# Two transformer blocks on one core: the differential-attention stage takes its norms by TensorE and one table, the sparse stage hands its roots to GpSimd

## The reference

```python
x = rms_norm(x, final_norm)                     # end of the first block
h = rms_norm_2(x, norm_mix[0])                  # directly behind it: a second norm of the result
q, k, v = split(h @ diff_w_in)                  # 8 heads; q and k normed in 64s, rotated
a = softmax(q1 k1) - lam * softmax(q2 k2)       # causal by chunks of 64
o = rms_norm_2(a @ v, subln_g) * (1 - lam_init); x = x + o @ diff_w_out
...
c_q, k, v, k_idx, w_idx = split(rms_norm_2(x, norm_mix[1]) @ dsa_w_in)
q = norm_rope(c_q @ w_uq); q_idx = rope(c_q @ w_uq_idx)
score = sum_h w_idx * relu(q_idx k_idx)         # masked
valid = top_k(score, 128)                       # per row; attention runs over these alone
```

## Time and profile before

| | |
|---|---|
| time, median of 3 runs | 2650.74 us (2647.53 to 2655.13) |
| the profiled execution: its own time, its span | 2656.82 us, 2654.7 us |
| PE busy | 2449.1 us, 92% |
| ACT, DVE, POOL busy | 906.6, 854.5, 1139.8 us |
| mean granted clock of TensorE | 0.958 |

### The profile page before, as it was taken

One profiled execution on the slowest core, in us unless ns is written; L12 is line 12 of the kernel. 1 busy time (PEld: TensorE's weight loads), 2 busy tenths in 40 slices (PEclk: granted clock), 3 DMA queues, 4 the chain that ended last, 5 costly groups with the idle time before them and its releaser, 6 DMA issues.

```text
span 2654.7 us, 27035 instructions
## 1 busy us (share of the span) xinstructions
PE 2449.1 (92%) x11136; PEld 1970.7 (74%) x11136; DVE 854.5 (32%) x1458; ACT 906.6 (34%) x1296; POOL 1139.8 (43%) x916
## 2 busy tenths in 40 slices
PE   7999999898887999999798679999999879999999
PEld 5888876687764788888586457888886657788887
DVE  3222117453123322200643733102024875420211
ACT  4222224221332422222554644313235245431331
POOL 6444434423631544444642125454454702444442
PEclk9999999989999999999898789999999889999999
DMA  4222222212310233222121003223321100232322
GB/s 134 96 95 95 96 95 72 72 32 98 124 65 16 95 95 95 96 95 96 64 79 64 1 21 91 95 96 99 103 80 65 64 33 17 70 105 96 96 95 79
DMA packets 148589, 210.66 MB, mean 79 GB/s; under 512 B 6121, under 2 KB 116978, under 8 KB 148466
## 3 DMA queue, kind: packets, MB, share of 16 engines
q1 hardware_dynamic: 148466, 208.93, 24.3%
HBM read 206.82 MB, written 2.10 MB: 79 GB/s over the span
## 4 chain that ended last, share of the span: by engine, by line
PE 75%; DVE 12%; ACT 5%; POOL 4%; issue 2%; DMA 2%; SPq 0%; POOLq 0%; ACTq 0%; DVEq 0%
PE ps L1248 22%; PE ps L1249 22%; PE ps L1250 22%; POOL wlo L711 2%; POOL sq L724 2%; PE ps L1865 1%; ACT whi L808 1%; DVE c_work L2528 1%; DVE c_best L2527 1%; PE ps L1841 1%; PE ps L1465 1%; PE ps L1851 1%; PE ps L1535 1%; PE ps L1302 1%; PE ps L1590 1%
## 5 line engine op out<-in xcount | busy, mean ns | idle before, releaser
L711 POOL TENSOR_TENSOR wlo<-raw,whi 128x512 fp32r<-128x512 f32 x776 | 1014.5, 1340 | 1327.2 <-ACT whi L808 1327.2
L808 ACT ACTIVATE whi<-raw 128x2048 fp32r<-128x2048 f32 (+1 forms) x195 | 371.2, 1905 | 779.4 <-DMA raw<-in_mlp_w 326.8
L1248 PE MATMUL ps<-hh,whi 128*128 128x512 f32 x1512 | 600.1, 397 | 26.7 <-DVE hl L1970 17.5
L1249 PE MATMUL ps<-hl,whi 128*128 128x512 f32 x1512 | 592.3, 392 | 0.0
L1250 PE MATMUL ps<-hh,wlo 128*128 128x512 f32 x1512 | 591.9, 391 | 0.0
L1248 PEld LDWEIGHTS ps<-hh,whi 128*128 128x128 f32 x1512 | 286.5, 189 | 104.1 <-issue 36.8
L1250 PE MATMUL ps<-gh,wlo 128*128 128x512 f32 x864 | 336.1, 389 | 0.0
L1248 PE MATMUL ps<-gh,whi 128*128 128x512 f32 x864 | 336.1, 389 | 0.0
L1249 PE MATMUL ps<-gl,whi 128*128 128x512 f32 x864 | 336.1, 389 | 0.0
L1249 PEld LDWEIGHTS ps<-hl,whi 128*128 128x128 f32 x1512 | 286.7, 190 | 59.8 <-issue 1.8
L1250 PEld LDWEIGHTS ps<-hh,wlo 128*128 128x128 f32 x1512 | 286.2, 189 | 60.2
(11 more groups left out here) (405 smaller groups left out, 2732.6 us busy)
## 6 DMA issues: line engine op xcount, KB each, us to landing
raw<-in_mlp_w SPq DMA_DIRECT2D x64, 1024.0 KB, 5.5
raw<-in_ffn_w_gate SPq DMA_DIRECT2D x22, 1024.0 KB, 5.1
raw<-in_ffn_w_up SPq DMA_DIRECT2D x22, 1024.0 KB, 5.2
raw<-in_ffn_w_down SPq DMA_DIRECT2D x22, 1024.0 KB, 4.8
raw<-in_w_in SPq DMA_DIRECT2D x13, 1024.0 KB, 5.2
raw<-in_diff_w_in SPq DMA_DIRECT2D x12, 1024.0 KB, 5.0
raw<-in_xattn_w_kv SPq DMA_DIRECT2D x8, 1024.0 KB, 5.0
raw<-in_dsa_w_in SPq DMA_DIRECT2D x8, 1024.0 KB, 4.9
```

The lines of the kernel that those rows point to most:

```text
L711: nc.gpsimd.tensor_tensor(wlo[i][:, c], raw[i][:, c], whi[i][:, c].bitcast(F32), ALU.subtract).then_inc(s_lo, 1)
L808: nc.scalar.activation(whi[i][:, 0:width(made[0])], raw[i][:, 0:width(made[0])], ACT.Copy)\
L1248: nc.tensor.matmul(dst, w_hi, x_hi, start=start, stop=False)
L1249: nc.tensor.matmul(dst, w_hi, x_lo, start=False, stop=False)
```

## The change

In the entry ACT loads one table set, which serves Ln and Exp, and squares each tile once, into eight tiles `a_xsq` of their own; POOL adds nothing there. PE sums the squares with 32 small matmuls whose moving side `gsq` has two columns, a one and the squared gain. Both norms come out of one Ln and one Exp on a 128x8 tile, since the second mean square follows from both sums. The factor as a tile of rows is made on PE, from `ident` scaled by it, right ahead of the first `turn_rows`, and DVE copies it to `rstd` after group 0; the 8 multiplications of `xT` come after group 3. In the attention `squares` and `row_sums` move ahead in step 1 and `factors` to step 2 of a head, and the turns of heads 6 and 7 move into the output projection. In the sparse stage the sum of squares on PE moves behind half of block b+1, the Newton step to POOL, two insertions of the query projection ahead of the loop, the block b+6 too, POOL splits b+9 before `scaled(2)`, and the mask takes one instruction. The diff, cut:

```diff
+Q_STEPS = (4, 9, 14, 19, 24, 29)
...
             def scaled(g, rows, gain):
 
-                pool.wait_ge(s_cst, g + 1)
+                y, w, u = c_rs[:, g, :], c_w[:, g, :], c_u[:, :]
+                pool.wait_ge(s_rrs2, g + 1)
+                if g:
+                    pool.wait_ge(s_cny, 4 * g)
+                nc.gpsimd.tensor_tensor(u, y, y, ALU.mult).then_inc(s_cny, 1)
...
+                nc.gpsimd.tensor_tensor(u, w, u, ALU.mult).then_inc(s_cny, 1)
+                nc.gpsimd.tensor_scalar(u, u, 1.5, None, ALU.add).then_inc(s_cny, 1)
+                nc.gpsimd.tensor_tensor(y, u, y, ALU.mult).then_inc(s_cny, 1)
+                pool.wait_ge(s_cny, 4 * g + 4)
...
                 scaled(1, c_rowb, "dsa_q_norm_2")
-                split_to(b + 8)
+                split_to(b + 9)
                 scaled(2, c_rowc, "dsa_q_norm_2")
...
-                split_to(b + 1)
-                e = E_DIFF
-                for t in range(1, KT):
-                    pool.wait_ge(s_esq, 8 * e + t + 1)
-                    if t > 1:
-                        pool.wait_ge(s_eacc, 7 * e + t - 1)
-                    first = sg[:, 0, :] if t == 1 else sq[:, 0, :]
-                    nc.gpsimd.tensor_tensor(sq[:, 0, :], first, sg[:, t % 4, :], ALU.add).then_inc(s_eacc, 1)
-                    pool.wait_ge(s_esq2, t + 1)
-                    if t > 1:
-                        pool.wait_ge(s_eacc2, t - 1)
-                    first = t1[:, 0, :] if t == 1 else sq[:, 1, :]
...
                     if p.entry == E_DIFF:
-                        if t >= 2:
-                            act.wait_ge(s_eacc2, max(t - 2, 1))
-                        nc.scalar.activation(t1[:, t % 2, :], xT[:, t, :], ACT.Square, scale=col("final_norm", t))\
-                            .then_inc(s_esq2, 1)
+                        nc.scalar.activation(a_xsq[:, t, :], xT[:, t, :], ACT.Square).then_inc(s_esq, 1)
...
                 prep_to(b + 1)
+                nc.scalar.preload_act_table_set(LN_SET)
                 entry(diff_entry)
                 prep_to(b + 2)
                 act.wait_ge(s_ehalf, E_DIFF + 1)
-                rsqrt(dr[:, 0:4], dr[:, 4:8], s_erstd)
-                act.wait_ge(s_f2, 1)
-                rsqrt(dr[:, 8:12], dr[:, 4:8], s_fr2)
-                act.wait_ge(s_fh, 1)
-                rsqrt(rstd[:, :], t1[:, 0, :], s_fr)
+                rsqrt(dr[:, 0:8], dr[:, 8:16], s_erstd)
                 act.wait_ge(s_rr, 1)
...
-                    if qt == 3 and h:
+                    if qt == 1 and h:
+                        squares(h - 1)
+                    if qt == 2 and h:
                         factors(h - 1)
                     if u < 29:
                         exponents(u + 3)
-                    if qt == 1 and h:
-                        squares(h - 1)
                     if u == 16:
                         prep_to(b + DIFF_BLOCKS + 1)
...
+                for st in range(2):
+                    put_rows(G_Q0, st, c_rowb[:, st, :], c_sq0)
                 put_rows(G_K0, 3, c_rowa[:, 3, :], a_sq, factor(3))
                 row_rstd2(0)
+                prep_to(b + 6)
...
-                    if v % 4 == 3:
-                        g, st = divmod(v // 4, ST)
+                    if v in Q_STEPS:
+                        g, st = divmod(2 + Q_STEPS.index(v), ST)
...
-                    if v in (7, 19):
-                        prep_to(b + 6 + v // 16)
-                turned(20, 4, lambda c: a_kT[:, c, :])
+                    if v == 20:
+                        prep_to(b + 7)
                 row_rstd2(1)
                 row_rstd2(2)
                 prep_to(b + 8)
+                turned(20, 4, lambda c: a_kT[:, c, :])
                 for st in range(ST):
                     put_rows(G_K1, st, c_rowa[:, st, :], a_sq, factor(st))
-                prep_to(b + 9)
+                    if st == 1:
+                        prep_to(b + 9)
...
-                rsqrt(c_rs[:, g, :], newton[:, 0, 0:32], s_rrs2)
+                rsqrt(c_rs[:, g, :], c_w[:, g, :], s_rrs2)
...
+                        if tail is not None and j == 0 and k == 6:
+                            tail()
...
-                pe.wait_ge(s_eacc, 7 * E_DIFF + 7)
-                pe.wait_ge(s_eacc2, 7)
+                pe.wait_ge(s_esq, 8 * E_DIFF + 8)
...
-                for i in range(2):
-                    for st in range(ST):
-                        c = 8 * i + 2 * st
-                        r = nc.tensor.matmul(ps[:, 7, c:c + 2], sq[:, i, ts(st, P)], ones[:, 0:2],
-                                             start=True, stop=True)
+                for st in range(ST):
+                    for t in range(KT):
+                        r = nc.tensor.matmul(ps[:, 7, 2 * st:2 * st + 2], a_xsq[:, t, ts(st, P)], gsq[:, t, :],
+                                             start=t == 0, stop=t == KT - 1)
...
-                nc.tensor.matmul(ps[:, 6, :], ones[:, :], sq[:, 0, :], start=True, stop=True).then_inc(s_ss, 1)
...
                         if g == 1:
-                            pe.wait_ge(s_fh, 1)
+                            pe.wait_ge(s_fdiag, 4)
+                            nc.tensor.matmul(ps[:, 6, :], ones[:, :], sq[:, 0, :], start=True, stop=True)\
+                                .then_inc(s_frow, 1)
+                            pe.wait_ge(s_fcopy, 1)
                         pe.wait_ge(s_rows, g)
                         turn_rows(4 * (g - 1), a_rows[:, (g - 1) % 2])
...
+                def last_heads():
+                    turn_out(6, 32)
+                    turn_out(7, 32)
+                    pe.wait_ge(s_dor, 8)
...
-                turn_out(6, 32)
-                turn_out(7, 32)
-                pe.wait_ge(s_dor, 8)
                 pe.wait_ge(s_de, 64)
-                project_out(b + DIFF_BLOCKS, upd, lambda k: (s_dhl, k + 1), o_h, o_l, 3)
+                project_out(b + DIFF_BLOCKS, upd, lambda k: (s_dhl, k + 1), o_h, o_l, 3, last_heads)
...
+                        if j == 1 and a == 1:
...
+                            for st in range(ST):
+                                r = nc.tensor.matmul(ps[:, 7, 2 * st:2 * st + 2], sq[:, 0, ts(st, P)],
+                                                     ones[:, 0:2], start=True, stop=True)
+                            r.then_inc(s_ess, 1)
...
+                use(b + 5)
+                for st in range(2):
+                    copied(G_K0, st)
+                    full(compressed(b + 5, 0, 1024, st, st), G_Q0, st)
...
-                half(dr[:, 4:8], ps[:, 7, 0:8:2], D, s_ehalf)
+                y, w, u = dr[:, 0:8], dr[:, 8:16], newton[:, 1, 0:8]
+                dv.done(V.tensor_scalar(w[:, 0:4], ps[:, 7, 0:8:2], -0.5 / D, -0.5 * EPS, ALU.mult, ALU.add))
+                dv.link(V.tensor_scalar(u[:, 0:4], ps[:, 7, 1:8:2], -0.5 / D, None, ALU.mult))
+                V.scalar_tensor_tensor(out=w[:, 4:8], in0=w[:, 0:4], scalar=EPS, in1=u[:, 0:4],
+                                       op0=ALU.mult, op1=ALU.add).then_inc(s_ehalf, 1)
                 dve.wait_ge(s_erstd, E_DIFF + 1)
-                r1, r2, w = dr[:, 0:4], dr[:, 8:12], dr[:, 4:8]
-                refine(r1, w, dr[:, 12:16])
-                dv.link(V.tensor_tensor(w, r1, r1, ALU.mult))
-                dv.link(V.tensor_tensor(w, w, ps[:, 7, 8:16:2], ALU.mult))
-                half(w, w, D, s_f2)
-                dve.wait_ge(s_ss, 8 * 2 + 1)
-                half(t1[:, 0, :], ps[:, 6, :], D, s_fh)
-                dve.wait_ge(s_fr2, 1)
-                refine(r2, w, dr[:, 12:16])
-                V.tensor_tensor(r1, r1, r2, ALU.mult).then_inc(s_rr, 1)
-                dve.wait_ge(s_fr, 1)
-                refine(rstd[:, :], t1[:, 0, :], t1[:, 1, :])
-                for t in range(KT):
-                    V.scalar_tensor_tensor(out=xT[:, t, :], in0=xT[:, t, :], scalar=col("final_norm", t),
-                                           in1=rstd[:, :], op0=ALU.mult, op1=ALU.mult).then_inc(s_x, 1)
+                dv.link(V.tensor_tensor(u, y, y, ALU.mult))
+                dv.link(V.tensor_tensor(w, w, u, ALU.mult))
+                V.scalar_tensor_tensor(out=y, in0=w, scalar=1.5, in1=y, op0=ALU.add, op1=ALU.mult).then_inc(s_rr, 1)
+                dve.wait_ge(s_rr, 1)
+                for st in range(ST):
+                    V.tensor_scalar(sq[:, 0, ts(st, P)], ident[:, :], dr[:, st:st + 1], None, ALU.mult)\
+                        .then_inc(s_fdiag, 1)
...
+                    if g == 0:
+                        dve.wait_ge(s_frow, 1)
+                        V.tensor_copy(rstd[:, :], ps[:, 6, :]).then_inc(s_fcopy, 1)
+                dve.wait_ge(s_fcopy, 1)
+                for t in range(KT):
+                    V.scalar_tensor_tensor(out=xT[:, t, :], in0=xT[:, t, :], scalar=col("final_norm", t),
+                                           in1=rstd[:, :], op0=ALU.mult, op1=ALU.mult).then_inc(s_x, 1)
...
-                    if qt == 2 and h:
+                    if qt == 1 and h:
```

(14 more changed lines are left out.)

59 lines of the change are left out of this document (33 added, 26 removed).

## The result

The changed kernel takes 2617.3 us, median of 4 runs (2613.0 to 2619.9), against 2649.9 (2647.5 to 2655.1): the ratio is 0.9873, with a 95% interval from 0.9851 to 0.9894. That is 32.6 us, where 51.7 were forecast, and the time is 1.3 us above the range of 2586 to 2616. The span of the profiled execution is 2617.2 us, 37.5 less.

What follows compares the result with a forecast made beforehand. PE, busy 92% of the span, was taken to bound the kernel. Entry and projection 21.7, attention 9.9, tail 5.1 and sparse attention 15.0 sum to 51.7 us off 2650.7, giving 2599.0, range 2586 to 2616.

## What to carry to other kernels

Where ACT alternates between two functions, look first for one table set that holds both: here the line with the preload was worth some 15 of 33 us. Before an insertion is moved out of a loop, read who waits for whom in the loop; if the engine that is relieved waits there anyway, the piece moved ahead of it is pure cost. And a long row of small matmuls is not priced by its first ones: in two lots with wide products between them the 64 records took 7.7 to 8.2 here, in one row 9.3 to 11.1.

## What the hardware showed beyond that

- A row of 2-column matmuls took the granted clock down with PE never idle, in all sixteen profiles that have it: 0.13 us each for the first 34, 0.22 for the last 30; 32 of them in a row took 3.9 us to the next product, 64 took 10.9 (9.3 to 11.1 over ten profiles).
- Equal code far from any change differs between executions: the mixing stage takes 167 to 171 or 174 to 175 us. The stretch through the sparse heads took 494.3 and 499.8 in two profiles of one kernel. The granted clock is all that tells them apart. The medians of single kernels move by about as much.
- The mask's operation on 128x256 took 2.5, 2.8 and 5.8 us beside an unbroken run on POOL, and each time ended within 0.5 us of the run's end; on 128x512 with POOL idle it took 0.43.
